# Split output projections, an earlier split at the expert borders and a shorter head in a two-layer hybrid decoder kernel

## What is computed

```
out = concatenate([att, y], axis=-1) @ w_out                    # mixer
mk, mv = split(mem @ w_ckv, 2)                                  # memory keys and values, also outputs
q = x @ w_cq ; p = softmax(q @ mk * d**-0.5) ; o = (p @ mv) @ w_co
out = out + _swiglu(x, w_exp_gu[e], w_exp_down[e]) * gate[..., e:e + 1]   # e = 0 .. 7
h = _layer_norm(ALPHA * h + part, ln_g, ln_b)
```

## Time and profile before

| | us |
|---|---|
| median of 3 runs | 1795.13 |
| lowest and highest | 1794.13, 1795.72 |
| profiled execution, its own time | 1792.82 |
| profiled execution, span from first to last instruction | 1790.7 |
| mean granted clock of TensorE | 0.993 |

### The profile page before, as it was taken

One profiled execution on the slowest core, in us unless ns is written; L12 is line 12 of the kernel. 1 busy time (PEld: TensorE's weight loads), 2 busy tenths in 40 slices (PEclk: granted clock), 3 DMA queues, 4 the chain that ended last, 5 costly groups with the idle time before them and its releaser, 6 DMA issues.

```text
span 1790.7 us, 23663 instructions
## 1 busy us (share of the span) xinstructions
PE 1743.2 (97%) x8760; PEld 1362.3 (76%) x8760; DVE 1214.5 (68%) x1659; ACT 845.4 (47%) x898; POOL 111.8 (6%) x120
## 2 busy tenths in 40 slices
PE   7999999999999999999999999999999999999998
PEld 4646487689999574558677888888888888888886
DVE  2687635255544287552715989899898989898994
ACT  1122211144442122212204777777777777777774
POOL 0630000000000252000001000000000000000000
PEclk9999999999999999999998999999999999999999
DMA  9556554855424445663672989899998989898980
GB/s 321 189 201 213 217 188 153 287 171 188 166 94 178 156 162 199 218 229 135 242 258 72 349 298 381 335 380 338 372 394 315 392 318 387 320 384 336 379 321 26
DMA packets 218514, 459.32 MB, mean 257 GB/s; under 512 B 10878, under 2 KB 49976, under 8 KB 218422
## 3 DMA queue, kind: packets, MB, share of 16 engines
q1 hardware_dynamic: 212710, 442.63, 68.3%
q0 software_dynamic: 3424, 11.50, 2.0%
q10 hardware_dynamic: 2304, 4.20, 0.6%
HBM read 444.97 MB, written 13.46 MB: 256 GB/s over the span
## 4 chain that ended last, share of the span: by engine, by line
PE 85%; DVE 7%; ACT 4%; issue 1%; DMA 1%; SPq 1%; POOL 0%; ACTq 0%; DVEq 0%; POOLq 0%
PE bank L1228 83%; PE bank L1232 3%; DVE arena L2701 1%; DVE ring_low L2170 1%; ACT high L1784 1%; DMA out<-mem_rows 1%; DVE R L2315 1%; ACT L1784 1%; ACT arena L1855 0%; POOL arena L972 0%; ACT ye_high L1823 0%; ACT SQ L1876 0%; DVE st L2673 0%; DVE st L2594 0%; SPq L734 0%
## 5 line engine op out<-in xcount | busy, mean ns | idle before, releaser
L2170 DVE TENSOR_TENSOR ring_low<-ring,high 128x2048 fp32r<-128x2048 f32 x264 | 598.7, 2288 | 81.3 <-ACT high L1784 80.5
L1784 ACT ACTIVATE high<-ring 128x2048 fp32r<-128x2048 f32 x264 | 505.1, 1918 | 141.8 <-PE bank L1228 137.6
L1228 PE MATMUL bank<-high,xg_high 128*128 128x512 f32 x704 | 278.1, 395 | 7.3 <-DVE ring_low L2170 7.0
L1228 PE MATMUL bank<-ring_low,xg_high 128*128 128x512 f32 x704 | 274.6, 390 | 0.0
L1228 PE MATMUL bank<-high,xg_low 128*128 128x512 f32 x704 | 274.2, 389 | 0.0
L1228 PEld LDWEIGHTS bank<-high,xg_high 128*128 128x128 f32 x704 | 132.2, 188 | 34.7 <-DVE ring_low L2170 8.4
L1228 PEld LDWEIGHTS bank<-ring_low,xg_high 128*128 128x128 f32 x704 | 132.2, 188 | 28.0
L1228 PEld LDWEIGHTS bank<-high,xg_low 128*128 128x128 f32 x704 | 132.3, 188 | 25.7
L1855 ACT ACTIVATE arena<-bank 128x512 f32<-128x512 f32 (+3 forms) x95 | 46.3, 525 | 217.1 <-PE bank L1228 141.5
L1228 PE MATMUL bank<-high,he_high 128*128 128x512 f32 x352 | 140.0, 398 | 0.0
L1228 PE MATMUL bank<-ring_low,he_high 128*128 128x512 f32 x352 | 137.4, 390 | 0.0
(11 more groups left out here) (327 smaller groups left out, 2578.0 us busy)
## 6 DMA issues: line engine op xcount, KB each, us to landing
ring<-in_w_exp_gu SPq DMA_DIRECT2D x176, 1024.0 KB, 9.9
ring<-in_w_exp_down SPq DMA_DIRECT2D x40, 2048.0 KB, 10.5
ring<-in_w_in SPq DMA_DIRECT2D x12, 2048.0 KB, 11.2
ring<-in_w_ffn_gu SPq DMA_DIRECT2D x22, 1024.0 KB, 8.7
ring<-in_w_ckv SPq DMA_DIRECT2D x8, 2048.0 KB, 9.1
ring<-in_cache_mem_k SPq DMA_DIRECT2D x16, 1024.0 KB, 8.1
ring<-in_cache_mem_v SPq DMA_DIRECT2D x16, 1024.0 KB, 6.6
ring<-in_cache_attn_k SPq DMA_DIRECT2D x32, 256.0 KB, 3.9
```

The costliest lines, as they stand in the source:

```text
L1228: return M.matmul(out, lhsT, rhs, start=start, stop=stop)
L1784: S.activation(high_bufs[h % HIGH_BUFS][:], ring[:, s, j * HALF:(j + 1) * HALF], ACT.Copy).then_inc(split_high, 1)
L2170: V.tensor_tensor(ring_low[:, s, part], ring[:, s, part], high_bufs[h % HIGH_BUFS][:], ALU.subtract).then_inc(split_low, 1)
```

## The change

It has five parts.

1. Head: the identity is loaded by itself, then x, then the query columns; constants, vectors, key columns, memory rows and page table follow. Seven of the small tensors go by POOL's queue, two (for layer 1) later. ACT empties two of the five x groups. The transposes of the vectors and of the memory rows are moved behind layer 0's key tiles. "dt" comes after the second query tile.
2. Mixer: the transposes run in the order tile 0, decode tile, tile 1; each group is taken as a high and a low part by ACT and DVE. The transposes of mem_k are moved ahead of the projection. w_out is split by ACT and DVE in four parts of 256 columns, the first two parts early, and PE forms three products each. The buffer mem_k is moved, and ACT's wait for the layer's stores comes earlier.
3. Cross attention: the cO blocks and the decode rows are split the same way, w_co too. DVE has four subtractions ahead of the copy after sPT and two parts of w_co ahead of oV's copies.
4. Three warming products stand ahead of each projection in place of two ahead of the mixer's.
5. Experts: the first half of chunk 1 is copied and subtracted before the loop goes round, ahead of ye_high and ye_low. The four scatter groups are each moved behind the next chunk.

```diff
 # head, SP
-            sp.dma_start(const[:], a["consts"]).then_inc(const_landed, 16)
...
+            sp.dma_start(const[:, C_ID:C_ID + P], a["consts"][:, C_ID:C_ID + P]).then_inc(ident_landed, 16)
...
                 columns((l, "q"), w_in, 0)
                 if l == 0:
...
+                    first_vectors()
+                columns((l, "k"), w_in, 512)
+                if l == 0:
+                    memory_rows()
+                for key, c0 in (("xbc0", 2048), ("xbc1", 2560)):
...
                 passed(sp, (l, "O", 1))
+                sp.wait_ge(stored, 16 * STORES_LAYER * (l + 1))
                 sp.dma_start(mem_k[:], o_mk[l, 0].rearrange("(t p) h d -> p t (h d)", p=P)).then_inc(mem_k_landed, 16)
 # weights of the two projections, ACT and DVE
+        def projection_high(act, l, what, n):
+            high, i, cols = projection_half(what, n)
+            rg.arrived(act, (l, what, i))
+            if n >= 2:
+                passed(act, (l, "m" if what == "out" else "co", 2 * n - 3))
+            nc.scalar.activation(high[:], projection_slot((l, what, i))[0][:, :, cols], ACT.Copy
+                                 ).then_inc(proj_high.sem, 1)
+
+        def projection_low(dve, l, what, n):
+            high, i, cols = projection_half(what, n)
+            w, w_low = projection_slot((l, what, i))
+            proj_high.wait(dve, l, projection_index(what, n))
+            nc.vector.tensor_tensor(w_low[:, :, cols], w[:, :, cols], high[:], ALU.subtract).then_inc(proj_low.sem, 1)
 # PE
+            def split_projection(l, what, name, x_hi, x_lo, src):
+
+                for n in range(4):
+                    high, i, part = projection_half(what, n)
+                    low = projection_slot((l, what, i))[1][:, :, part]
+                    for m in range(2):
+                        cols = slice(m * P, (m + 1) * P)
+                        bk = turns.open(pe, (l, name, 2 * n + m))
+                        if m == 0:
+                            if n == 0:
+                                warm(bk, 3)
+                                copied(pe, src)
+                            proj_low.wait(pe, l, projection_index(what, n))
                         for k in range(KT):
+                            last = product(bk[:, 0:T], high[:, k, cols], low[:, k, cols], x_hi[:, k, :], x_lo[:, k, :],
+                                           k == 0, k == KT - 1)
                         full(last)
...
-                columns_of((l, "out", 0), (l, "m"), 0, mixT, (l, "mixT", 4))
-                columns_of((l, "out", 1), (l, "m"), 4, mixT)
+                blocks8((l, "mixT"), mix, MIX_BLOCKS, lambda t: mix_ready.wait(pe, l, NORM_ORDER.index(t)))
                 pe.wait_ge(mem_k_landed, 16 * (l + 1))
                 for i in range(4):
                     bk = turns.open(pe, (l, "mkT", i))
...
+                split_projection(l, "out", "m", mixT_high, mixT_low, (l, "mixT", 4))
                 norm_sums(l, 0, "m")
...
                 copied(pe, (l, "cO", 3))
-                copied(pe, (l, "soT"))
-                columns_of((l, "co", 0), (l, "co"), 0, oT)
-                columns_of((l, "co", 1), (l, "co"), 4, oT)
+                split_projection(l, "co", "co", oT_high, oT_low, (l, "soT"))
 # PE, experts
-                    if 2 * f < KT:
-                        scatter_before(f)
+                    if f and 2 * (f - 1) < KT:
+                        scatter_before(f - 1)
 # ACT, experts
-            def high_part(e, c, p, after=None):
+            def high_part(e, c, p, halves=(0, 1), after=None):
...
                 for j, h in halves_of(p):
+                    if j not in halves:
+                        continue
                     if after is not None:
                         half_used(act, after, c, HALVES - HIGH_BUFS + h)
...
                 for p in range(1, NGU + NDN):
-                    high_part(e, c, p)
+                    high_part(e, c, p, (1,) if p == 1 else (0, 1))
...
                 with act.If(e < EXPERTS - 1):
                     high_part(e + 1, c, 0, after=e)
+                    high_part(e + 1, c, 1, (0,), after=e)
                 act.wait_ge(dn_done, i * NDN + NDN)
 # ACT, mixer
                 memory_part(5)
+                act.wait_ge(stored, 16 * STORES_LAYER * (l + 1))
+                for n in range(2):
+                    projection_high(act, l, "out", n)
                 memory_part(6)
 # DVE, cross attention
                 V.tensor_scalar(sP[0:32], sP[0:32], rr1[0:32], None, ALU.mult).then_inc(cs_probs.sem, 1)
+                for i in range(4):
+                    o_high.wait(dve, l, i)
+                    bk = take(dve, (l, "cO", i))
+                    emptied_after((l, "cO", i), V.tensor_tensor(
+                        oT_low[:, 2 * i:2 * i + 2, 0:NP_TOK], bk[:].rearrange("p (j n) -> p j n", j=2),
+                        oT_high[:, 2 * i:2 * i + 2, 0:NP_TOK], ALU.subtract))
                 bk = take(dve, (l, "sPT"))
...
+                for n in range(2):
+                    projection_low(dve, l, "co", n)
 # DVE, experts
                 with dve.If(e < EXPERTS - 1):
                     low_part(e + 1, c, 0)
+                    low_part(e + 1, c, 1, (0,))
                 dve.wait_ge(dn_done, i * NDN + NDN)
```

More of the change, by code:

```diff
@@ L488, in build @@
         convT = R
-        mixT = SQ
+        mixT_high = parts_in("mixT_high", "SQ", 0, [KT, T])
+        mixT_low = parts_in("mixT_low", "arena", 3 * 1024, [KT, T])
+        out_high = [parts_in(f"out_high{j}", "arena", at, [KT, GU]) for j, at in enumerate((6 * 1024, share))]
         sqf = SQ[:, :, :].rearrange("p k t -> p (k t)")
@@ L1005, in _, with projection_half, projection_index, projection_slot @@
             pool.wait_ge(mem_stored, 16 * 8 * L)
+        def projection_half(what, n):
+            i, h = divmod(n, 2)
+            return (out_high if what == "out" else co_high)[h], i, slice(h * GU, (h + 1) * GU)
+        def projection_index(what, n):
+            return (0 if what == "out" else 4) + n
+        def projection_slot(key):
+            s = rg.pos[key] % RING
+            return tuple(x[:, s, :].rearrange("p (k n) -> p k n", k=KT) for x in (ring, ring_low))
+        def projection_high(act, l, what, n):
[10 more added lines that the diff above has]
+            nc.vector.tensor_tensor(w_low[:, :, cols], w[:, :, cols], high[:], ALU.subtract).then_inc(proj_low.sem, 1)
         ffn_chunks = [(0, "gu", f) for f in range(NGU)] + [(0, "dn", i) for i in range(NDN)]
@@ L1243, in slot, with blocks8 @@
                 return ring[:, rg.arrived(pe, key), :]
-            def blocks8(name, src, wait=None):
-                for n in range(5):
-                    t = n // 2
+            def blocks8(name, src, blocks, wait=None):
+                for n, (t, half) in enumerate(blocks):
                     rows = TILES[t][1]
@@ L1692, in parts @@
                         return high, ring_low[:, s, part]
-                    def product(out, w, w_low, xh, xl, first, last):
-                        mm(out, w, xh, first, False)
-                        mm(out, w, xl, False, False)
-                        return mm(out, w_low, xh, False, last)
                     for f in range(NGU):
@@ L2027, in _ @@
                 memory_part(7)
-                act.wait_ge(stored, 16 * STORES_LAYER * (l + 1))
+                for n in (1, 2, 4):
+                    t, bk = MIX_BLOCKS[n][0], take(act, (l, "mixT", n))
+                    t0, rows = TILES[t]
+                    for j in range(4):
+                        at = ((4 if t == 2 else 0) + j) * rows
+                        ins = S.activation(mixT_high[:, 4 + j, t0:t0 + rows], bk[:, at:at + rows], ACT.Copy,
+                                           scale=cols_ssm(l)[:, j:j + 1])
+                    ins.then_inc(mix_high.sem, 1)
                 for i in range(4):
@@ L2032, in _ @@
                              lambda bk: bk[:].rearrange("p (j n) -> p j n", j=2))
+                for n in range(2, 4):
+                    projection_high(act, l, "out", n)
                 norm(l, 0)
@@ L2281, in residuals @@
                     residual(l, name, m)
+                    if m in (1, 3):
+                        projection_low(dve, l, "co" if i else "out", 2 + m // 2)
                     copied(dve, (l, name, m))
```

215 lines of the change are left out of this document (133 added, 82 removed).

## The result

The changed kernel takes 1815.44 us (median of 5 runs, 1814.93 to 1817.71) against 1795.72 (5 runs, 1794.13 to 1797.69): the ratio is 1.0111, with a 95% interval of 1.0096 to 1.0126. The forecast was 1813.5. The profiled execution after is the median itself, with a span of 1813.7; that of before, 1792.82, lay 2.3 under its median.

The account below looks back on a forecast made before the run. PE was taken to bound the kernel (85% of the chain of waits). Terms 19.3 + 7.5 - 4.7 - 3.7 = 18.4 on 1792.8 gave 1811.2, plus 2.3 for the runs' median 1813.5, range 1806 to 1821.

Parts of the forecast that it names:

- Borders, +19.3: Expert borders: early copy waits for a seventeenth count, from the next expert's chunk 0; 2.75 us lost at each of seven.
- Mixer projection, +7.5: Mixer, two layers: products save 5.35 each, but PE stalls for mem_k's load and the clock drops; ends 0 and 11.
- the clock's price: Mixer projection: one lower-clock stretch of about 3.5 us after the idle, a loss of 1.75 a layer.
- 6.2 and 7.6 us: Mixer, layers 0 and 1: PE idle after the mixer transposes until mem_k's keys land at 228.4 and 799.7.
- Cross projection, -4.7: Cross attention, two layers: 5.35 less on PE, minus 2.05 for DVE's subtractions and 0.9 for warming; between -2 and -7.
- the clock loss here stays as it is: Cross projection: the time lost to the lower clock was taken as unchanged, so no term for it.
- Head, -3.7: Head: earlier first query tile and no router wait, less the moved transposes and a slower clock; between -1 and -6.
- I take 5.3, as POOL's small loads now share that time: Head: first query tile 5.3 us earlier, from 4.2 for 1.6 MB less loaded ahead and at most 2.6 for issues.
- The tiles may start at the lower clock, 0 to 1.75; 0.5: Head: query tiles possibly starting at the lower clock, a loss of 0 to 1.75 us, taken as 0.5.
- The border works as meant: Rival, expert borders: early copy starts as the down products end, -2.5 in seven, total 1791.7; chance 0.08.
- The keys are there in time: Rival, mixer projection: no stall, both layers keep their 5.35, -10.7 in place of +7.5, total 1795.3; chance 0.06.
- The delay goes on: Rival, expert borders: DVE has little slack behind the moved additions, 4.5 a border, 31.5, total 1826; chance 0.06.

Follow-up runs that it names:

- best2: Changed kernel with mended border count, first scatter group between chunk 1's halves, mem_k transposes behind projection, ten warming products there, sixteen head fillers: 1787.04 us (0.9956).
- small_late: Changed kernel, with POOL issuing its seven small loads only when the query columns have landed: 1817.39 us (1.0123).
- border_count: Changed kernel, one wait altered: the early copy of chunk 1's first half waits for the previous expert's last down product, not a seventeenth count: 1801.09 us (1.0035).
- keys_behind: Changed kernel with the transposes of mem_k put back behind the mixer's output projection: 1811.57 us (1.0093).
- best1: Changed kernel with mended border count, first scatter group between chunk 1's halves, mem_k transposes behind projection, seventeen warming products there, sixteen head fillers: 1789.85 us (0.9968).
- head_warm: Changed kernel with sixteen filler products (identity by identity) in PE's wait for the query columns: 1817.13 us (1.0125).

## Why the prediction was right, and where it was not

The sum was 18.4, the traces differ by 23.0, and the forecast came within 1.9 of the median because the 2.3 added for the profiled execution did not return: after lies on its median. That closeness is luck, and so is part of the sum: the head is 5.8 over its term and the mixer 2.9 under.

**Borders, +19.3:** 19.6 (7 x 2.80). Count, order of ACT's work and three waits came as derived; 1.61, 1.36 and 0.21 are shown for 1.8, 1.7 and 0.4, as the page counts the drain of the last product as busy.

**Mixer projection, +7.5:** 4.6. The mechanism holds, and the clock's price too (3.68 for 1.75, so 1.9 a layer). The mis-sized term is the stall, "6.2 and 7.6 us": PE idled 5.15 in either layer. I had put the load's issue where the trace of before had it. There the store ahead of it was under way for 2.8 in layer 0 and 4.2 in layer 1 (from 220.69 to 223.50 and from 790.59 to 794.80); now it took 2.0 both times; why it landed sooner was not settled. Its two issues before:

```profile
220.69 0.34 ACTq L1972 DMA_DIRECT2D out<-mem_rows  x1
...
790.59 0.34 ACTq L1972 DMA_DIRECT2D out<-mem_rows  x1
```

The Trainium skill's rule that I leaned on (TensorE: Matmul & The Clock Gate, the section on why this matters for your kernels) agrees with the rows: 0.50 behind the idle of 5.15, and in best2, where fillers leave no such idle, a clock of 1.00 throughout the mixer's projection of both layers.

**Cross projection, -4.7:** -4.7. The copy after sPT came 2.27 behind its transposes (0.35 before), with the four subtractions (2.47) ahead of it, and the warming products cost 0.7 (0.9 said). But "the clock loss here stays as it is" holds in size only, and by luck. Before, it fell in the projection (30.42 for 28.75). After, it falls in the 64 products against the values (8.67 for 7.07, granted 0.50 from 336 to 339), which now stand behind PE's longer wait for that copy, and the projection runs at 1.00.

**Head, -3.7:** +2.1 in this pair of traces, between -0.8 and +6.8 with the other four of the same head: the step that failed. None of the five lies within its range of -1 to -6. "I take 5.3, as POOL's small loads now share that time" was 2.1: I had priced those loads by their bytes, and six of them held 2 MB up by 3.4 us (16.45 against 13.06; 2.7 to 4.5 with the other four). "The tiles may start at the lower clock, 0 to 1.75; 0.5" was 2.4 (1.4 and 1.0 in the first two tiles), because the sixteen transposes that had kept PE busy in that wait had been moved away, and with fillers in their place the tiles run at full speed. The transposes cost 2.2 (2.05 said), the router's wait of 0.9 went as said, and a wait of 0.5 for DVE's pair_in came on top: -2.1 - 0.9 + 2.4 + 2.2 + 0.5 = 2.1.
The Trainium skill (DMA: Bandwidth & Descriptors, the section on issuing engines not being separate DMA queues) states that DMAs of all issuing engines run on the same sixteen DMA engines and interleave; small_late agrees, with 385 for 133 GB/s.

**Not in the sum:** +0.6 between the stages and +0.8 in the tail, where the last 20 transposes took 4.58 instead of 3.04 (3.03 in border_count, whose code is the same there).

**The rivals.** "The border works as meant" was made by border_count: the early copy stands at 1076.1, but the border gives +0.15, not -0.36, since two short waits cost as much as one longer one. "The keys are there in time" did not happen; its aside, that DVE's copies come next, is what keys_behind shows. "The delay goes on" did not happen: 101.03, not 102.7.

## What to carry over

A wait on a count is worth deriving: which instruction adds the last unit, and whether that instruction stands before or after the work that the wait is meant to overtake. Work moved out of a wait may have to be replaced by something that keeps PE busy, and work moved into a wait may bring its own producer's store and load with it. A small load is priced by what it does to the large one beside it.

## What was not expected of the hardware

**Half speed at a granted clock of 1.00.** In the head the windows show 1.00 throughout (17 to 18 us, above), yet sixteen records take 3.64 in the changed kernel and 1.92 behind fillers. So in the first 20 us the column does not tell the level; the products' durations do. The Trainium skill (TensorE: Matmul & The Clock Gate, Part 1 on the clock gate) has the slow level as the default, which activity releases; the durations agree, the column does not show it.

**Two waits cost more than their idle.** The visible waits of a border grew from 1.00 to 3.18, by 2.18, and the expert by 2.80: each further stop of the stream of 512-column products costs some 0.3 beside the idle that is shown. border_count agrees: one stop more than before, 0.16 less idle, 0.15 more for the expert.

**The clock goes with differences as large as the edits.** Ten runs of border_count lie between 1794.3 and 1807.7, with mean granted clocks of 0.989 and 0.984, while the five of the changed kernel lie within 2.8. The profiled one is the fastest of the ten, which is why its trace agrees with the expectation and the median does not. best1's ten runs go from 1784.2 at 0.995 to 1797.7 at 0.988. That the clock makes all of such a difference is not shown, only that the two go together. Where the lower clock falls differs from one trace to another with the same instructions: 0.50 from 227 to 233 and from 336 to 339 us in the changed kernel, and in head_warm also from 348 to 354. What decides about it was not settled here.
